# Product-key retrieval on VectorE: 112 of 256 sums searched per head, positions decoded two heads at a time

## What is computed

```python
s1 = jnp.einsum('bshd,kd->bshk', q[..., 0, :], sk[0])     # 8 heads, 128 keys
s2 = jnp.einsum('bshd,kd->bshk', q[..., 1, :], sk[1])
v1, i1 = lax.top_k(s1, 16)                                # sorted, largest first
v2, i2 = lax.top_k(s2, 16)
cand = v1[..., :, None] + v2[..., None, :]                # 16 x 16 sums
cand_idx = i1[..., :, None] * 128 + i2[..., None, :]
top_s, top_pos = lax.top_k(cand, 16)                      # over all 256
expert_idx = take_along_axis(cand_idx, top_pos)
gates = softmax(top_s)
u = take(expert_down, expert_idx); v = take(expert_up, expert_idx)
y = (gelu(h . u) * gates) . v                             # 16,384 experts exist
```

## Time and profile before

| | |
|---|---|
| Median of 3 executions | 2028.86 us (2027.82 to 2030.07) |
| The profiled execution's own time | 2029.63 us |
| Its span, first to last instruction | 2027.8 us |
| Mean granted TensorE clock | 0.996 |
| TensorE busy | 1997.4 us |
| VectorE, GpSimd, ScalarE busy | 1366.6, 1198.0, 804.1 us |

### The profile page before, as it was taken

How to read it: one execution, slowest core, us unless ns; L and a number is a source line. 1 busy time by engine, 2 the same in 40 slices (tenths; PEclk the granted TensorE clock), 3 DMA queues, 4 the chain that set the end, 5 groups by cost and what they waited for, 6 DMA issues and landing times.

```text
span 2027.8 us, 28865 instructions
## 1 busy us (share of the span) xinstructions
PE 1997.4 (99%) x10185; PEld 1762.0 (87%) x10185; DVE 1366.6 (67%) x2241; ACT 804.1 (40%) x1074; POOL 1198.0 (59%) x650
## 2 busy tenths in 40 slices
PE   7999999999999999999999999999999999999997
PEld 6888888887887888999999999999888888888886
DVE  6424242334723399899997887873797888888946
ACT  5222222223533333333334666665434333333352
POOL 5342434243245233878887655555899888888821
PEclk9999999999999999999999999999999999999998
DMA  6231323233233322888898878888999999999921
GB/s 214 75 117 61 114 62 113 59 118 94 73 94 105 114 74 83 288 302 322 311 326 310 297 300 303 296 303 299 335 386 385 369 358 368 356 361 370 356 63 42
DMA packets 167335, 455.00 MB, mean 224 GB/s; under 512 B 13265, under 2 KB 62417, under 8 KB 165457
## 3 DMA queue, kind: packets, MB, share of 16 engines
q1 hardware_dynamic: 58032, 209.04, 30.6%
q0 software_dynamic: 36864, 134.23, 17.2%
q10 hardware_dynamic: 72352, 110.64, 15.9%
HBM read 396.71 MB, written 54.53 MB: 223 GB/s over the span
## 4 chain that ended last, share of the span: by engine, by line
PE 95%; DVE 3%; ACT 1%; DMA 0%; issue 0%; ACTq 0%; DVEq 0%; SPq 0%
PE bank L845 29%; PE bank L847 29%; PE bank L846 29%; PE bank L1084 4%; PE bank L952 1%; PE bank L1034 1%; PE bank L1019 1%; DVE h_lo L1420 0%; PE bank L995 0%; PE bank L1005 0%; DVE bank L1239 0%; ACTq L728 0%; PE bank L921 0%; ACT b_hi L538 0%; DMA xT<-x_cols 0%
## 5 line engine op out<-in xcount | busy, mean ns | idle before, releaser
L448 POOL TENSOR_TENSOR w_lo<-raw,w_hi 128x1024 fp32r<-128x1024 f32 x390 | 938.2, 2413 | 717.0 <-ACT w_hi L494 713.4
L845 PE MATMUL bank<-h_hi,w_hi 128*128 128x384 f32 (+1 forms) x1552 | 560.4, 361 | 3.7 <-DVE h_lo L1420 3.1
L847 PE MATMUL bank<-h_hi,w_lo 128*128 128x384 f32 (+1 forms) x1552 | 548.6, 353 | 0.0
L846 PE MATMUL bank<-h_lo,w_hi 128*128 128x384 f32 (+1 forms) x1552 | 548.3, 353 | 0.0
L494 ACT ACTIVATE w_hi<-raw 128x1024 fp32r<-128x1024 f32 x390 | 407.5, 1057 | 181.0 <-PE bank L847 61.9
L845 PEld LDWEIGHTS bank<-h_hi,w_hi 128*128 128x128 f32 x1552 | 292.2, 188 | 25.4 <-DVE h_lo L1420 4.8
L847 PEld LDWEIGHTS bank<-h_hi,w_lo 128*128 128x128 f32 x1552 | 291.9, 188 | 21.2
L846 PEld LDWEIGHTS bank<-h_lo,w_hi 128*128 128x128 f32 x1552 | 292.3, 188 | 19.9
L847 PE MATMUL bank<-w_hi,b_lo 128*128 128x512 f32 x768 | 298.8, 389 | 0.0
L846 PE MATMUL bank<-w_lo,b_hi 128*128 128x512 f32 x768 | 298.8, 389 | 0.0
L845 PE MATMUL bank<-w_hi,b_hi 128*128 128x512 f32 x768 | 298.8, 389 | 0.0
(11 more groups left out here) (184 smaller groups left out, 2568.1 us busy)
## 6 DMA issues: line engine op xcount, KB each, us to landing
raw<-weights SPq DMA_DIRECT2D x390, 512.0 KB
act_scratch<-scr ACTq DMA_DIRECT2D x64, 384.0 KB
gate_scratch<-scr ACTq DMA_DIRECT2D x12, 2048.0 KB
scr<-gate_scratch ACTq DMA_DIRECT2D x22, 768.0 KB
scr<-act_scratch ACTq DMA_DIRECT2D x22, 768.0 KB
xT<-gate_scratch ACTq DMA_DIRECT2D x10, 768.0 KB
xT<-act_scratch ACTq DMA_DIRECT2D x10, 768.0 KB
scr<-scr ACTq DMA_DIRECT2D x20, 128.0 KB, 2.5
```

The costliest lines, as they stand in the source:

```text
L448: return nc.gpsimd.tensor_tensor(w_lo[:, s, :], raw[:, s % RAW, :], w_hi[:, s, :].bitcast(F32), ALU.subtract)
L845: nc.tensor.matmul(out, a_hi, c_hi, start=first, stop=False)
L846: nc.tensor.matmul(out, a_hi, c_lo, start=False, stop=False)
L847: return nc.tensor.matmul(out, a_lo, c_hi, start=False, stop=last)
```

## The change

The sums of rows 0 to 3 are built with all 16 columns (64), those of rows 4 to 15 with columns 0 to 3 (48), together 112 per token. The instructions that build them now cover all four token tiles: two per head in place of four. `best` searches 112 elements in place of 256. A position in the list of 112 is decoded by `rows_and_columns`, eight instructions for one or two heads: below 64 the row is `pos >> 4` and the column `pos & 15`; from 64 on the row is `(pos >> 2) - 12` and the column `pos & 3`. `decode` loses the two shifts and the cast. The number and the places of the dot products, of the fetches and of the waits between engines are as before.

```diff
--- before.py
+++ after.py
@@ -140,6 +140,9 @@
 RAW_Q = 4
 
 NPAIR = PH * TOPK
+WIDE_ROWS, NARROW = 4, 4
+NWIDE = WIDE_ROWS * TOPK
+NCAND = NWIDE + (TOPK - WIDE_ROWS) * NARROW
 U_SLOTS = 4
 V_SLOTS = 6
 PLAIN_HEADS = 4
@@ -256,13 +259,14 @@
 
         s12 = cut(5632, 4096).rearrange("p (m t k) -> p m t k", m=8, t=TT)
         taken = cut(1024, 1024).rearrange("p (t k) -> p t k", t=TT)
-        cand = cut(0, 1024).rearrange("p (t k) -> p t k", t=TT)
+        cand = cut(0, TT * NCAND).rearrange("p (t k) -> p t k", t=TT)
         val = cut(9728, 1024).rearrange("p (t m k) -> p t m k", t=TT, m=2 * PH)
         idx = cut(10752, 1024).bitcast(U32).rearrange("p (t m k) -> p t m k", t=TT, m=2 * PH)
         top = cut(2048, 512).rearrange("p (t h k) -> p t h k", t=TT, h=PH)
-        pos = cut(2560, 512).bitcast(U32).rearrange("p (t h k) -> p t h k", t=TT, h=PH)
-        posu = cut(3072, 128).bitcast(U32).rearrange("p (t a k) -> p t a k", t=TT, a=2)
-        posf = cut(3200, 128).rearrange("p (t a k) -> p t a k", t=TT, a=2)
+        pos = cut(2560, 512).bitcast(U32).rearrange("p (h t k) -> p h t k", t=TT, h=PH)
+        posu = cut(5120, 512).bitcast(U32)
+        posf = cut(3072, 512)
+        row_col = cut(5120, 256).rearrange("p (h t a k) -> p h t a k", h=2, t=TT, a=2)
         pick = cut(0, 2048).rearrange("p (n j) -> p n j", j=TOPK)
         sel_s = cut(11776, 1024).rearrange("p (t a n) -> p t a n", t=TT, a=2)
         gate_s = cut(3584, 512).rearrange("p (t n) -> p t n", t=TT)
@@ -1455,17 +1459,31 @@
                 each(lambda src, rest, v, p: nc.vector.max(v[:, 8:16], rest), more > 3)
                 each(lambda src, rest, v, p: nc.vector.max_index(p[:, 8:16], v[:, 8:16], rest), more > 4)
 
+            def rows_and_columns(h, nh):
+
+                ps = pos[:, h:h + nh, :, :]
+                n = TT * nh * TOPK
+                u = [posu[:, n * c:n * c + n].rearrange("p (h t k) -> p h t k", t=TT, h=nh) for c in range(4)]
+                f = [posf[:, n * c:n * c + n].rearrange("p (h t k) -> p h t k", t=TT, h=nh) for c in range(4)]
+                together([lambda: ts(u[0], ps, 4, None, ALU.logical_shift_right),
+                          lambda: ts(u[1], ps, 2, None, ALU.logical_shift_right),
+                          lambda: ts(u[2], ps, TOPK - 1, None, ALU.bitwise_and),
+                          lambda: ts(u[3], ps, NARROW - 1, None, ALU.bitwise_and)])
+                step(nc.vector.tensor_copy(posf[:, 0:4 * n], posu[:, 0:4 * n]))
+                row, column = row_col[:, 0:nh, :, 0, :], row_col[:, 0:nh, :, 1, :]
+                step(stt(out=row, in0=f[1], scalar=float(WIDE_ROWS - NWIDE // NARROW), in1=f[0], op0=ALU.add, op1=ALU.max))
+                step(stt(out=f[2], in0=row, scalar=float(WIDE_ROWS), in1=f[2], op0=ALU.is_lt, op1=ALU.mult))
+                step(tt(column, f[2], f[3], ALU.max))
+
             def decode(h):
 
                 more = h > 0
                 at = slice(TOPK * h, TOPK * h + TOPK)
                 sel = sel_s[:, :, :, at]
-                together([lambda: ts(posu[:, :, 0, :], pos[:, :, h, :], 4, None, ALU.logical_shift_right),
-                          lambda: ts(posu[:, :, 1, :], pos[:, :, h, :], TOPK - 1, None, ALU.bitwise_and),
-                          lambda: nc.vector.tensor_copy(idx_p.rearrange("p (t a k) -> p t a k", t=TT, a=2),
-                                                        idx[:, :, 2 * h:2 * h + 2, :])])
-                step(nc.vector.tensor_copy(posf, posu))
-                together([lambda: tt(pick, posf.rearrange("p t a k -> p (t a k)").unsqueeze(2).to_broadcast([P, P, TOPK]),
+                step(nc.vector.tensor_copy(idx_p.rearrange("p (t a k) -> p t a k", t=TT, a=2),
+                                           idx[:, :, 2 * h:2 * h + 2, :]))
+                rc = row_col[:, h % 2 if h < PH - 2 else 0].rearrange("p t a k -> p (t a k)")
+                together([lambda: tt(pick, rc.unsqueeze(2).to_broadcast([P, P, TOPK]),
                                      iota_p[:, 0:TOPK].unsqueeze(1).to_broadcast([P, P, TOPK]), ALU.is_equal)], more)
                 p4 = pick.rearrange("p (n k) j -> p n k j", k=TOPK)
                 i4 = idx_p.rearrange("p (n j) -> p n j", j=TOPK).unsqueeze(2).to_broadcast([P, 2 * TT, TOPK, TOPK])
@@ -1476,22 +1494,27 @@
 
             for m in range(2 * PH):
                 if m >= 2 * PLAIN_HEADS and m % 2 == 0:
-                    decode(m - 2 * PLAIN_HEADS)
-                    if m < 2 * PH - 2:
-                        decode(m - 2 * PLAIN_HEADS + 1)
+                    h, nh = m - 2 * PLAIN_HEADS, 2 if m < 2 * PH - 2 else 1
+                    rows_and_columns(h, nh)
+                    for d in range(nh):
+                        decode(h + d)
                 ve.wait_ge(s12_ready, m + 1)
                 best([(s12[:, m % 8, t, :], taken[:, t, 0:P], val[:, t, m, :], idx[:, t, m, :]) for t in range(TT)],
                      4 if m >= 2 * PLAIN_HEADS else 0)
                 ve.sem_inc(s12_free, 1)
                 if m % 2 == 1:
                     h = m // 2
-                    together([lambda t=t: tt(cand[:, t, :].rearrange("p (a b) -> p a b", a=TOPK),
-                                             val[:, t, m - 1, :].unsqueeze(2).to_broadcast([P, TOPK, TOPK]),
-                                             val[:, t, m, :].unsqueeze(1).to_broadcast([P, TOPK, TOPK]), ALU.add)
-                              for t in range(TT)])
-                    best([(cand[:, t, :], taken[:, t, :], top[:, t, h, :], pos[:, t, h, :]) for t in range(TT)],
+                    together([lambda x=x: tt(x[0], val[:, :, m - 1, x[1]:x[2]].unsqueeze(3).to_broadcast([P, TT, x[2] - x[1], x[3]]),
+                                             val[:, :, m, 0:x[3]].unsqueeze(2).to_broadcast([P, TT, x[2] - x[1], x[3]]),
+                                             ALU.add)
+                              for x in ((cand[:, :, 0:NWIDE].rearrange("p t (a b) -> p t a b", a=WIDE_ROWS),
+                                         0, WIDE_ROWS, TOPK),
+                                        (cand[:, :, NWIDE:NCAND].rearrange("p t (a b) -> p t a b", b=NARROW),
+                                         WIDE_ROWS, TOPK, NARROW))])
+                    best([(cand[:, t, :], taken[:, t, 0:NCAND], top[:, t, h, :], pos[:, h, t, :]) for t in range(TT)],
                          5 if h >= PLAIN_HEADS else 0)
 
+            rows_and_columns(PH - 1, 1)
             decode(PH - 1)
 
             def next_dots(n):
```

## The result

| | before | after |
|---|---|---|
| Median | 2029.46 us (4 executions) | 2044.26 us (4 executions, 2043.61 to 2046.01) |
| Ratio | | 1.0075, 95% interval 1.0063 to 1.0086 |
| Profiled execution, its span | 2029.63, 2027.8 us | 2046.01, 2044.2 us |

Forecast were 2028.8 us, 2026.5 to 2032.0, and no change. The changed kernel lies 12 us above the upper end. Its profiled execution is the slowest of the four; so the times taken from its trace lie near the upper end of what the change costs.

A forecast was written before the change was run, and what follows sets the result against it. TensorE was taken to bound the kernel. VectorE's -24.0 (search), -6.2 (sums) and +9.0 (decoding) made -21 us busy but 0 on the path; from the 2028.9 median, less 0.1, came 2028.8 us, range 2026.5 to 2032.0.

The forecast's parts named there:

- The sums: Building the sums on VectorE: from 25.9 to 19.7 us busy, 6.2 less, with waiting kept at 1.8 a head.
- Waits and queues: Step on hand-overs between engines in the selection: no wait added, and the first fetch's 0.98 us wait goes.
- From there on dot products wait for rows: After dot 0, VectorE's saving becomes idle time ahead of line 1199, growing from 31.3 by about 20 us.
- The sequence behind each wait is late by nothing: After each VectorE wait for a row, work starts when it did before, since the wait ends then: no delay.
- GpSimd waits for VectorE less: GpSimd's waits for VectorE, 2.00 us at 1056.36 and 5.01 at 1109.60 before, were to shrink.
- my 2.5 us of holds: Per decoding call, one hold of 0.9 us and one of 1.6; 12.5 us in all, decoding 23.3.
- slack of the queue: GpSimd's 5.01 us wait at 1109.60 was taken to show slack, as TensorE ran on through it.
- four holds of 2.41 in each call: Upper bound for the decoding on VectorE: 48.2 us of holds, net +44.7 us.
- the path is put at 0: Effect on the time: 0, as TensorE's products cover the selection without a gap; without cover, at most 21 us.
- The slower one: Rival: the call ahead of decode(7) makes `sel_ready` late, TensorE stands 4.3 us at line 1103, 2033.2 us; chance 0.06.
- My room of 6.5 us at the end: Ahead of the last dot before the softmax: head 7 saves 3.0 in search, 2.9 in sums, plus 0.62 waiting.
- The rule on the shared ports: VectorE and GpSimd lock shared ports; with two-input instructions held each time, VectorE's sum is +14.5 us, not -21.

The follow-up runs named there:

- run 1: Kernel before with only the search cut from 256 to 112 sums: 2028.71 us, ratio 0.9994.
- run 2: Changed kernel with the old decoding put back, new sums and search of 112 kept: 2029.71 us, ratio 1.0000.
- run 8: Changed kernel with the decoding block's intermediate values in PSUM, one more cast and an added wait ahead of the first block: 2030.81 us, ratio 1.0002.
- run 7: Changed kernel with the decoding block of heads 2 and 3 moved ahead of the first dot product: 2039.56 us, ratio 1.0053.
- run 9: Changed kernel with a dot product moved into only the two pair blocks (heads 2 and 3, 4 and 5): 2037.64 us, ratio 1.0040.
- run 6: Changed kernel with one existing dot product moved behind the cast in each of the last four decoding blocks: 2029.26 us, ratio 0.9994.
- run 11: Changed kernel with one input of the expert numbers' instruction copied to PSUM first, block unchanged: 2029.71 us, ratio 1.0002.
- run 13: Kernel before with 28 unused MAX8 ahead of decoding heads 2 and 4, and one expert-number input in PSUM: 2032.89 us, ratio 1.0016.
- run 3: Changed kernel with the old sums and search of 256, only the new decoding kept: 2054.89 us, ratio 1.0122.
- run 10: Kernel before with 14 unused MAX8 (3.1 us) ahead of decoding heads 2 and 4: four executions 2026.99 to 2029.51, five 2037.74 to 2041.63 us.

## Why the prediction was wrong

**What held.** TensorE bounds the kernel and the search saves what was worked out: the 160 instructions take 258 to 269 ns and their busy time falls from 60.8 to 36.8 us, the 24.0 forecast. With the search alone nothing was gained, and the saving showed as waiting for rows (runs 1 and 2). The sums came to 12.1 us, not 19.7, as the holds in them were fewer. The idle time ahead of the dot products grew, from 29.2 to 58.3 us, but 21.8 of these stand at the first row, ahead of the gaps that matter. VectorE's total fell by 2.5 us, not 21.

**The step that failed** is under "Waits and queues": "From there on dot products wait for rows", "The sequence behind each wait is late by nothing", and "GpSimd waits for VectorE less". I costed the block as busy time on an engine that waits elsewhere, and took its cover to be that waiting. But the block lies between two dot products, where VectorE doesn't wait; there, GpSimd waits for VectorE, with four slots, and everything in its queue with it. The question for each gap was: how long until the next dot product? It could be worked out from my own terms. The 5.3 us, less the old shifts and cast that stood in them (2.5 + 0.2 + 0.2), leave 2.4; the block of a pair adds 2.2 unhindered. That is 4.6 us without holds, 7.1 with my 2.5 us of holds and 14.2 with the bound's four. It was 13.0. I read the 5.01 us wait at 1109 as slack of the queue. It was slack for one wait, not for 44 us of them.

**The size that failed** is the hold: "four holds of 2.41 in each call" was meant as a bound for one instruction each. Single instructions took 5.2 and 5.6 us, since a late GpSimd runs lower halves in pairs. The row of 5.38 us for four sums already held more than one. The block took 32.8 us in all where I had 23.3 (within the bounds), the expert numbers 19.4 where I had left 14.1. But the price of a hold decides nothing as long as the path is put at 0: with its upper bound the sum would have given the same time.

**The rivals.** The slower one had the right end of the chain and too little of it. The softmax was late, but what stood was ScalarE at the exponential (6.0 us) with the GELU behind it, and so TensorE 5.5 us, not line 1103; I had 4.3. The 6.1 us before that, through weights loaded late, and the 4.9 us of busy time at a lower granted clock were in no rival. My room of 6.5 us at the end was counted from a row that would come at 1080.1; by then the rows were late themselves. The rule on the shared ports in the Trainium skill, "SBUF — State Buffer", section "SBUF: two separate sides", pointed the right way; these runs bear it out (run 8: no SBUF pair, no hold). By it VectorE's sum was +14.5 us, and I left the path at 0 all the same; against GpSimd's own holds I set its 717 us of idle time, of which only 31.5 lay between 808 and 1130 us.

**What stays open.** How the 16.4 us divide among the gaps was not measured one by one; runs 7 and 9 give a third for one pair's block and some 8 us for the two single ones, and three edits that differ (runs 6, 8 and 11) each take away the whole, so shares can't be added up. The share of the loop is open, as said under runs 11 and 13. The later stage has VectorE's line 1607 at 208.5 us where it was 187.2; it isn't on TensorE's path and wasn't looked into.

## What to carry to other kernels

Where an engine hands back buffers at fixed places of a hand-written order, the stretch between two of those places is the quantity to watch, not the engine's total: work taken off elsewhere pays for work put there only in part (10 of 25 us by run 3). Before adding a block, ask who waits at the next hand-over and what is queued behind that wait; here, moving one dot product into each of four blocks was worth 15 us. And look for loops, as these rows suggest one: if being late makes the other engine's work come in one piece, and that piece holds you, a small delay grows.

## What the hardware showed that I had not expected

- The same program can have two times with nothing changed: 2027 to 2030 or 2038 to 2042 us (run 10). A loop that either starts or doesn't would explain it; no trace of the upper group was taken.
- VectorE's holds are not limited to one GpSimd instruction: an instruction of 64 elements, 0.22 us when free, took 5.24 us, out just behind a fetch and two lower halves on end (4.78 us). The Trainium skill, "SBUF — State Buffer", section "SBUF: two separate sides", has the loser blocked for the other's whole instruction; the rows show it blocked for two in a row, and passed by instructions that GpSimd began after it. With one input in PSUM none of the block's instructions took more than 0.43 us.
- An idle time of 5.5 us on TensorE was followed by 15 products at the 1.2 GHz level in 4.9 us, one of 2.8 us by 12 of them in 3.75 us.
